# Row tiles split in row order and moved to the transposed layout by DMA transposes

## What is computed

```python
h = rmsnorm(x, norm_g)                       # (t, 1024)
u = h @ w_in                                 # (t, 11 * 256), eleven splits of 256 channels
a_b, a_c, a_x, a_g, b_v, b_a, b_g, c_u, c_g, x_q, x_g = split(u, 11)
y_a = a_b * conv3(a_c * a_x) * silu(a_g)     # causal, per channel
y_b = silu(layernorm(conv31(b_v * sigmoid(b_a)) + bias)) * silu(b_g)
y_c = (pooled_means(c_u) - c_u) @ pool_w ... * silu(c_g)
y_x = attention(x_q, 256 memory tokens, 4 heads) * silu(x_g)
out = rmsnorm(x + concat(y_a, y_b, y_c, y_x) @ w_out, final_norm_g)
```

## Time and profile before

| what | value |
|---|---|
| median of 3 runs | 1610.9 us |
| profiled execution, its own time | 1610.67 us |
| its span | 1608.9 us |
| TensorE busy (matmuls) | 1519.9 us, 94% |
| VectorE busy | 1118.2 us, 70% |
| ScalarE busy | 533.5 us, 33% |
| GpSimd busy | 195.1 us, 12% |
| DMA moved | 216.00 MB, 134 GB/s over the span |
| granted TensorE clock | 0.981 of full speed |

### The profile page before, as it was taken

How to read it: one execution, slowest core, us unless ns; L and a number is a source line. 1 busy time by engine, 2 the same in 40 slices (tenths; PEclk the granted TensorE clock), 3 DMA queues, 4 the chain that set the end, 5 groups by cost and what they waited for, 6 DMA issues and landing times.

```text
span 1608.9 us, 33113 instructions
## 1 busy us (share of the span) xinstructions
PE 1519.9 (94%) x12262; PEld 1322.2 (82%) x12262; DVE 1118.2 (70%) x3067; ACT 533.5 (33%) x1122; POOL 195.1 (12%) x164
## 2 busy tenths in 40 slices
PE   5678899999999999999999999999999999999976
PEld 4567788888888888888888888888888888888865
DVE  6678594958668494958768494957768494957653
ACT  7455333223322333223322332323322332323322
POOL 0011011111111011111101011111101011111100
PEclk9889999999999999999999999999999999999998
DMA  9603723434160523434150423434160423434036
GB/s 278 178 6 129 293 103 131 156 117 169 49 235 3 181 106 130 156 117 169 47 228 12 175 112 130 156 117 169 41 234 12 178 109 130 156 117 164 24 131 218
DMA packets 83171, 216.00 MB, mean 134 GB/s; under 512 B 7369, under 2 KB 33149, under 8 KB 83133
## 3 DMA queue, kind: packets, MB, share of 16 engines
q1 hardware_dynamic: 83133, 215.50, 36.9%
HBM read 189.42 MB, written 26.05 MB: 134 GB/s over the span
## 4 chain that ended last, share of the span: by engine, by line
PE 44%; DVE 31%; issue 17%; ACT 3%; DMA 2%; SPq 2%; DVEq 1%; ACTq 0%; POOL 0%
DVE z L1061 14%; PE u L428 7%; PE u L430 7%; PE u L429 7%; PE qps L428 4%; PE qps L430 4%; PE qps L429 4%; PE sps L428 3%; PE sps L430 3%; PE sps L429 3%; DVE pt_lo L1091 2%; DVE probs L1083 2%; ACT probs L773 2%; PE u L443 2%; DVE st L1069 1%
## 5 line engine op out<-in xcount | busy, mean ns | idle before, releaser
L428 PE MATMUL u<-h_hi,w_hl 128*128 128x256 f16 (+1 forms) x2992 | 791.9, 270 | 4.1 <-ACT yc L883 2.7
L429 PE MATMUL u<-h_lo,w_hl 128*128 128x256 f16 (+1 forms) x2992 | 790.8, 270 | 0.0
L430 PE MATMUL u<-h_hi,w_hl 128*128 128x256 f16 (+1 forms) x2992 | 790.6, 270 | 0.0
L1061 DVE SCALAR_TENSOR_TENSOR z<-glu,cst,z 128x256 f32<-128x256 f32 (+1 forms) x1020 | 421.6, 482 | 0.5
L428 PEld LDWEIGHTS u<-h_hi,w_hl 128*128 128x128 f16 x2992 | 294.6, 99 | 47.3 <-issue 6.4
L430 PEld LDWEIGHTS u<-h_hi,w_hl 128*128 128x128 f16 x2992 | 294.6, 99 | 33.2
L429 PEld LDWEIGHTS u<-h_lo,w_hl 128*128 128x128 f16 x2992 | 294.7, 99 | 32.2
L715 ACT ACTIVATE gate<-u,inv 128x256 f32<-128x256 f32 (+1 forms) x204 | 83.6, 461 | 255.9 <-PE u L430 254.8
L428 PE MATMUL sps<-ring,y_hi 128*128 128x512 f32 (+1 forms) x280 | 111.6, 399 | 15.1 <-DVE ring L1103 14.8
L1394 POOL TENSOR_TENSOR sa<-cu 128x540 f32<-128x540 f32 (+1 forms) x17 | 30.7, 1804 | 708.3 <-ACT cu L715 708.3
L1008 DVE TENSOR_TENSOR h_lo<-u,h_hi 128x512 f16<-128x512 f32 (+1 forms) x66 | 41.7, 672 | 105.7 <-ACT h_hi L732 105.7
(11 more groups left out here) (186 smaller groups left out, 1992.7 us busy)
## 6 DMA issues: line engine op xcount, KB each, us to landing
ring<-wo_split SPq DMA_DIRECT2D x256, 512.0 KB, 6.3
ob<-in_x_prompt SPq DMA_DIRECT2D x34, 512.0 KB, 4.2
out<-ob SPq DMA_DIRECT2D x32, 512.0 KB, 3.3
xb<-in_x_prompt SPq DMA_DIRECT2D x30, 512.0 KB, 4.3
w_hl<-in_w_in SPq DMA_DIRECT2D x20, 512.0 KB, 7.2
wo_split<-ring SPq DMA_DIRECT2D x16, 512.0 KB, 5.4
probs<-in_w_out SPq DMA_DIRECT2D x8, 256.0 KB, 5.7
stage<-in_w_mem_k SPq DMA_DIRECT2D x8, 128.0 KB, 4.8
```

The lines of the kernel that those rows point to most:

```text
L428: nc.tensor.matmul(out, a_hi, b_hi, start=first, stop=False)
L429: nc.tensor.matmul(out, a_hi, b_lo, start=False, stop=False)
L430: return nc.tensor.matmul(out, a_lo, b_hi, start=False, stop=last)
L1061: ins = nc.vector.scalar_tensor_tensor(z[:, c, 0:n], glu[:, c, k:k + n], w, z[:, c, 0:n], ALU.mult, ALU.add)
```

## The change

All tiles of x but the first two (those of chunk 0) change their way; none of them is transposed on TensorE. Its fp16 halves are made in row order into a new buffer `row16` (128 x 2 x 1024): `row_hi` on ScalarE copies xb to the high half in one instruction, `row_lo` on VectorE subtracts. Then `row_across` on SP issues two DMA transposes, one to h_hi and one to h_lo, each for 128 x 1024 fp16 elements (256 KB). There is one `row16` for both tiles, so row_hi waits until the other tile's transposes have landed (`rows_in`). The next chunk's b_a waits for `rows_in` in place of `h_lo_ok`.

The order moves too. Tile 0's halves are made at the start of a chunk (row_hi before the b_a sigmoid, row_lo before `normalise`), from a tile that was loaded, squared and scaled at the end of the chunk before (`after`). Its transposes are issued behind ring piece 8. Tile 1 is loaded before that (at piece 7), squared before `mix` on ScalarE, scaled behind `zt` on VectorE; its halves are made during the out projection, after tile 0's transposes have landed. SP waits for its row_lo behind ring piece 12, loads the following tile into xb, and then issues tile 1's transposes, ahead of pieces 13 to 15. The following tile's square, rsqrt and scaling stand before the last squares on ScalarE and before add_half(1) on VectorE.

To have room, `zt` shares the memory of `sa` (so POOL waits for `zs_ok`), the staging of w_out in chunk 0 has three buffers for four (`RAW`), and the scratch for descriptors is 512 for 1024. The slots t0 to t3 leave the PSUM rotation but for the first two tiles, which are transposed on TensorE as before.

```diff
 SLOTS = ["b_a", "b_v", "x_q", "c_u", "a_c", "a_x", "a_b", "a_g", "mix", "b_g", "zf", "c_g", "x_g",
-         "zb", "t0", "t1", "t2", "t3"]
+         "zb"]
...
-RAW, WST, RING = 4, 4, 8
+RAW, WST, RING = 3, 4, 8
...
-        zt = sb("zt", [P, 2, GW])
+        zt = sa[:, :, :].rearrange("p a b -> p (a b)")[:, 0:2 * GW].rearrange("p (t c) -> p t c", t=2)
+        row16 = sb("row16", [P, 2, D], F16)
...
+            def row_across(t, m):
+                for half, dst in enumerate((h_hi, h_lo)):
+                    sp.dma_start(dst[:, :, t * P:t * P + m], row16[0:m, half, :],
+                                 transpose=True).then_inc(rows_in[t].sem, 16)
...
                 if first:
+                    sp.wait_ge(row_lo_ok.sem, 1)
+                    sp.dma_start(xb[:, :], x_next).then_inc(x_in.sem, 16)
                     sp.wait_ge(pt_ready.sem, 2)
...
-                    if q == 8 and x_next is not None:
-                        v = NFIRST - 2 if type(i) is int and i == 0 else i * len(SLOTS) + NFIRST - 2
-                        sp.wait_ge(u_ready.sem, v)
+                    if q == KT - 1 and x_next is not None and not first:
+                        sp.wait_ge(row_lo_ok.sem, row_lo_ok.at(i, 1))
                         sp.dma_start(xb[:, :], x_next).then_inc(x_in.sem, 16)
+                    if q == KT and rows:
+                        if x_next is None:
+                            sp.wait_ge(row_lo_ok.sem, row_lo_ok.at(i, 1))
+                        if first:
+                            sp.wait_ge(o_piece.sem, 1)
+                        row_across(0, rows[0])
+                    if q == KT + 4 and len(rows) > 1:
+                        sp.wait_ge(row_lo_ok.sem, row_lo_ok.at(i, 2))
+                        sp.dma_start(xb[0:x_after.shape[0], :], x_after).then_inc(x_in.sem, 16)
+                        row_across(1, rows[1])
...
+            def row_hi(i, j, t, m):
+                act.wait_ge(x_scaled.sem, j + 1)
+                if t:
+                    act.wait_ge(rows_in[0].sem, rows_in[0].at(i, 32))
+                elif needed(rows_in[1].at(i, 0)):
+                    act.wait_ge(rows_in[1].sem, rows_in[1].at(i, 0))
+                nc.scalar.activation(row16[0:m, 0, :], xb[0:m, :], ACT.Copy).then_inc(row_hi_ok.sem, 1)
...
+            def row_lo(i, j, t, m):
+                dve.wait_ge(row_hi_ok.sem, row_hi_ok.at(i, t + 1))
+                nc.vector.tensor_tensor(row16[0:m, 1, :], xb[0:m, :], row16[0:m, 0, :],
+                                        ALU.subtract).then_inc(row_lo_ok.sem, 1)
```

More of the change, by code:

```diff
@@ L205, in encoder_program @@
         h_hi_ok, h_lo_ok = signal("h_hi_ok", 4), signal("h_lo_ok", 4)
+        row_hi_ok, row_lo_ok = signal("row_hi_ok", 2), signal("row_lo_ok", 2)
+        rows_in = [signal(f"rows_in{t}", 32) for t in range(2)]
         u_ready = signal("u_ready", len(SLOTS))
@@ L463, in project @@
                 if name == ORDER[0]:
-                    pe.wait_ge(h_lo_ok.sem, h_lo_ok.at(i, 4 if n == N else 2))
+                    if type(i) is int and i == 0:
+                        pe.wait_ge(h_lo_ok.sem, 4)
+                    else:
+                        for t, _, _ in tiles(n):
+                            pe.wait_ge(rows_in[t].sem, rows_in[t].at(i, 0))
                 for c in range(CT):
@@ L823, in kw, with chunk @@
                 nc.scalar.activation(wo_hi[:, k % WST, :], raw[:, b, :], ACT.Copy).then_inc(kw_hi.sem, 1)
-            def chunk(i, n, nxt):
+            def chunk(i, n, row0=None, row1=None, after=None):
                 first = type(i) is int and i == 0
@@ L838, in chunk @@
                     act.wait_ge(v_l.sem, 2)
+                if row0 and not first:
+                    row_hi(i, *row0)
                 scaled_out(i, n, "b_a", gate[:, 0, :, 0:n], ACT.Sigmoid, sig_ok)
@@ L846, in chunk @@
                 prepare(1)
-                if nxt:
-                    squares(nxt[0][1], nxt[0][3], i)
+                if first:
+                    squares(row0[0], row0[2])
                 scaled_out(i, n, "x_q", dq_hi[:, :, 0:n], ACT.Copy, q_hi)
@@ L908, in chunk @@
                         piece_hi(q)
-                if len(nxt) > 1:
-                    squares(nxt[1][1], nxt[1][3], i)
+                if row1:
+                    row_hi(i, *row1)
                 if first:
@@ L915, in chunk @@
                     keys_values_hi(1)
-                if len(nxt) > 1:
-                    rows_hi(i, nxt[1][0], *nxt[1][1:])
+                if after:
+                    squares(after[0], after[2], i)
                 nt = len(tiles(n))
@@ L950, in _, with next_tiles @@
             w_squares(3)
[L952 to L959, removed]
+            def next_tiles(i):
+                return (2 * i + 4, 0, P), (2 * i + 5, 1, P), (2 * i + 6, 0, P)
+            chunk(0, N, *next_tiles(0))
+            with act.Fori(1, LAST - 1) as i:
+                chunk(i, N, *next_tiles(i))
+            chunk(LAST - 1, N, *next_tiles(LAST - 1)[0:2], (2 * LAST + 4, 0, SAMPLE))
+            chunk(LAST, N, (2 * LAST + 4, 0, SAMPLE))
+            chunk(CHUNKS, SAMPLE)
         @block.vector
@@ L1122, in chunk @@
                     dve.wait_ge(hist_ok.sem, hist_ok.at(i, 3))
-                if not first and nxt:
+                if row0 and not first:
+                    row_lo(i, *row0)
                     normalise(i - 1, N)
```

138 lines of the change are left out of this document (62 added, 76 removed).

## The result

The changed kernel takes 1645.2 us (median of 4 runs, 1637.7 to 1648.1) against 1611.0 us before (4 runs, 1610.6 to 1611.4): a ratio of 1.0205, with a 95% interval of 1.017 to 1.024. It is slower by 2%, and its runs differ by 10 us where those of before agree within 1. The profiled execution took 1642.96 us, its span is 1641.2. The forecast of 1576 was wrong in sign, though the time lies in the wide range.

What follows compares the result with a forecast made beforehand. TensorE was taken as the bound (busy 89.90 of 90.70 us), with VectorE's chain nearly as long in a chunk's first 55 us. 1610.67 - 27.9 - 0.6 - 8.8 + 3 = 1576.4 us; range 1566 to 1750, if faster 1568 to 1590.

Steps and rivals of the forecast that it cites:

- TensorE's part: Transposes before the out projection (1.07 us) and in half 1 (0.79) leave PE: 27.9 us, plus about 0.6 for the last.
- VectorE's part: The chain from `glu` to the taps shortens by at least 2.9 us, `glu` 0.4 later; PE's z_rows wait goes, 8.8 us.
- The third piece's y_lo: Out projection: PE arrives 1.07 us earlier, with 0.2 us of room before this input; priced nothing, at most 0.3 a chunk.
- Stall of 0 behind the transposes: Out projection: four transposes, each holding SP 0.52 us, are hidden; piece 13 lands at 16.8, wanted at 17.8.
- the rule in the prediction (15.25 + 3s): Landing time of ring piece 13 after the out projection's first matmul, s being SP's hold per transpose; stall starts at s = 0.85.
- the prediction's own check: Out projection, in bytes: 1 MB more takes 2.5 us, loads end at 17.5 instead of 15.0; last piece wanted at 20.5.
- held queue: Rival, pieces 13 to 15: each transpose holds SP or the queue much longer than 0.52 us; 1722 at s = 4.09; chance 0.22.
- Chunk 0, +3 us with bounds 0 and 8: Three staging buffers of w_out for four, and SP waiting for row_lo at piece 12, add 3 us; bounds 0 and 8.

Runs made afterwards that it cites:

- late_across: The changed kernel with SP's wait for tile 1's row_lo, the following xb load and tile 1's transposes moved from behind piece 12 to behind piece 15: 1594.1 us.
- one_block: The changed kernel with each DMA transpose moving one 128x128 block instead of eight, order and waits kept: 1592.9 us.
- plain: The changed kernel with each DMA transpose replaced by a plain copy of the same 256 KB in 256-byte runs, order and waits kept: 1608.1 us.
- xb_early: The changed kernel with chunk 0's wait for tile 0's row_lo and next xb load put ahead of SP's wait for the last weight halves: 1631.1 us.
- raw3: The kernel before with three staging buffers for w_out in chunk 0 instead of four, nothing else: 1617.6 us.
- early_late_last: The changed kernel with xb_early and late_across together, and the sample tile's transposes in the last prompt chunk also behind piece 15: 1582.1 us.
- four_stages: early_late_last with chunk 0's fourth staging buffer for w_out back, in the memory of the squares' throw-away output: 1577.7 us.

## Why the prediction was wrong

**TensorE's part: right.** L443's work is gone but for the 16 transposes of the first two tiles, and where nothing else holds PE the period is 87.75 us (late_across, one_block). Against 90.59 this is 2.84 us, where the prediction had 1.86 + 0.63 = 2.5. Over 14 periods that is 40 us, and it was there to be had.

**VectorE's part: right.** No wait at z_rows is left. The `glu` step starts 10.75 us after b_a's first matmul (763.55 and 752.80), and 10.69 before (738.76 and 728.07): the 0.4 us that I gave it are 0.06. The third piece's y_lo shows no wait.

**Stall of 0 behind the transposes: the failed step in the steady chunks.** Two sizes in it were off, both the same way. SP is held 1.33 us by the high half's transpose and 2.69 by the low one's, for 0.52; the 0.52 was read at 1.68 us in the earlier trace rows, among the first loads of the kernel, not in an out projection. (The landing was not off where it was used: the second transpose of tile 0 lands 4.3 us after its issue.) And the engines: all packets of the queue take 42.5% of 16 engines over 1641.2 us in the changed kernel, 36.9% over 1608.9 before; the difference, 103.8 us over 62 transposes, is 1.67 us each, where 2.5 / 4 = 0.63 was assumed from the ring's rate.

```profile
q1 hardware_dynamic: 147581, 231.50, 42.5%
```

By the rule in the prediction (15.25 + 3s), s = 2.0 makes piece 13 late by 3.4 us; measured is 3.25 us of period. That agreement is luck. Piece 13 goes out at t = 15.3 to 16.1 and lands at 19.1 to 20.8, which is 1.3 to 3.0 late, since it needs about 4 to 5 us and not 6.3. The waits on record are 28.8 us in 14 periods, 2.06 each; the fallen clock costs, as an estimate, 1.45 us in 7 of them (b_a's start less 21.9 and the wait, with a fall against without), 0.7 on average; 0.4 to 0.5 is in neither. The same rule gives plain (s = 0.63) no stall, and it has 1.25 us; it gives one_block (s = 1.17) 1.0 us, and it has none.

The amount of work for the engines fits all of them. The prediction checked it against the last piece, wanted at t = 20.5, with 2.5 us for the four transposes. The DMA share of one out projection, first of the kernel before (20 us), then of the changed kernel, plain, one_block and late_across (24 us each), from t = 0:

```profile
705.29:725.29 20.00, 20.00 (x96) 16.65 (x94) 6.99 (x17) 4.56 (x10) 3.83 (x3) 1.00 0.61 236
728.99:752.99 24.00, 22.53 (x101) 17.92 (x100) 7.53 (x16) 5.58 (x10) 3.82 (x3) 1.00 0.82 240
714.70:738.70 24.00, 23.53 (x111) 18.93 (x110) 8.58 (x18) 5.59 (x10) 3.83 (x3) 1.00 0.76 240
710.89:734.89 24.00, 24.00 (x118) 19.77 (x117) 9.11 (x21) 5.94 (x11) 3.86 (x3) 1.00 0.59 202
706.06:730.06 24.00, 24.00 (x118) 19.77 (x117) 7.98 (x17) 5.59 (x10) 3.86 (x3) 1.00 0.77 240
```

| kernel | engines' time (us) | more than before | loads done by estimate, 15.0 + that | last piece lands, 14 chunks | PE's waits for pieces |
|---|---|---|---|---|---|
| changed | 19.7 | 7.5 | 22.5 | 22.1 to 23.2 | 28.8 |
| plain | 18.2 | 6.0 | 21.0 | 20.5 to 21.9 | 12.0 |
| one_block | 14.2 | 2.0 | 17.0 | 18.2 to 19.5 | none |
| late_across | 18.5 | 6.3; tile 0's half is ahead of the pieces | 18.2 | 17.3 to 19.6 | none |

So four transposes take 7.5 us of all engines there, not 2.5. With the right size the prediction's own check gives a last piece that is 2 us late, with no word on SP. SP's being held may in part be the same thing seen from the other side: in plain three ring loads hold it 3.88 us, where the same three in the changed kernel take 1.47. That SP has a part of its own is not excluded, and no run takes it away alone. The order then decides who pays: in the changed kernel pieces 13 to 15 stand directly behind the xb load and two transposes, where the prediction had one us of room. The rival "held queue" named the place, and said that the gain is gone at s = 1.7. It has an s of 2.0, and 0.4 us a chunk is lost; its mechanism, SP alone, is not what the runs bear out.

0.262 MB in 1.67 us of all engines are 157 GB/s. The Trainium skill ("DMA: Bandwidth & Descriptors", Latency and other measured facts) has 261 GB/s or more. That is an effective bandwidth, and this is the engines' packet time beside other traffic, so the two needn't be the same thing; the measurement decides here. The Trainium skill's 1309 ns for one 128x128 block ("VectorE: DVE Perf Modes", The three transpose paths) is near the 1.11 to 1.22 us that SP is held for one here, while its landing takes 2.4 us at least. Eight blocks don't cost eight of them by either measure.

**Chunk 0, +3 us with bounds 0 and 8: the failed step with the largest price.** It is +21.4, or +20.0 without the scatter ahead of the first statistics. Its parts, as the runs show them: 10.2 us by the load of xb (xb_early), 5.4 by what stands ahead of pieces 13 to 15 (late_across), 6.5 by the buffer (raw3; 5.7 from early_late_last to four_stages). Together they give back 18.8 of the 20.0 us of the first period, to 100.68. The 5.4 aren't the transposes alone: late_across also moves SP's wait for row_lo of tile 1 (nothing is issued from 187.1 to 190.3 us in the changed kernel) and the xb load, and one_block, with an eighth of each transpose in the same place, gains 1.2. I had priced the buffer and one wait of SP. What I missed is `squares` of tile 1 on ScalarE. In the steady chunks it stands ahead of the mix copy too, but on a tile that has landed 17 us earlier (694.67 and 711.49). In chunk 0 the same line stands behind a load that SP issues after the last weight half. Everything behind it on ScalarE waits, and PE with it. What is queued behind each wait was named for the loop and not for its first turn.

**The sample.** I had nothing for it; it is +4.9 us. In the last prompt chunk its two transposes hold SP 2.7 us ahead of piece 9, which is issued at t = 11.7, lands at 16.0 and is wanted at 12.3; PE waits 3.47 us there. Moving them behind piece 15 gives back 4.3 (76.99 to 72.71).

Together: 21.4 + 5.7 + 4.9 + 0.3 = 32.3, the difference of the spans.

## What to carry to other kernels

Work that leaves the bounding engine for the DMA queue is not free where that queue has a deadline. Add up the time that the engines need until the last deadline, with a price for the new kind of transfer that allows for short runs (here three times that of the ring's bytes), ask which transfers stand directly behind it, and issue what is wanted last, last: one line was worth 51 us of 1645. Where a loop is peeled, follow a moved wait through the first and the last turn separately, since a load that is long there in the loop may be the next thing SP gets to in chunk 0.

## What the runs showed of the hardware

- A DMA transpose from SBUF to SBUF held SP for at least 1.09 us with one block and 1.23 us with eight. The second of a pair of eight blocks held it 1.3 to 3.8 us in the changed kernel and up to 4.7 in late_across. A plain copy of the same bytes and runs held it 0.61 or 0.67.
- For 256 KB it took 1.67 us of all 16 engines over the whole execution, and 1.9 in the out projection (7.5 us for four); a plain copy in runs of 256 bytes took 1.35 (42.2% of 1605.6 us) and 1.5.
- It landed 4.2 to 6.6 us after its issue on the queue that it shares with ring loads, and up to 9.6 where the pair stands right behind all ring pieces (late_across); eight blocks take 0.8 us more than one (medians 4.9 and 4.1).
- A transpose on ScalarE's queue beside the ring loads on SP's queue took up to 18.9 us to land, and 15 in the chunk shown, where tile 0's low half on SP's queue took 4.3.
- PE idle for 12 us in chunk 0 was at half clock in that stretch (0.50); from 152 to 180 us the clock was 0.92 and from 180 to 210 us 0.83, where those of before had 1.00. In the steady chunks 3.4 us at 0.50 stood behind 7 of 14 waits. So a stall of PE can cost more than its length. It also goes with the spread of the changed kernel's runs: 1637.7 us at a mean clock of 0.969, 1647.4 at 0.961.
